# MLP down products of a two-layer decoder: pairs of output tiles by Strassen's seven block products over eight of eleven k tiles

## The chip, the cores and the metric

One core of one Trainium2 chip runs one program. The metric is the device time of one execution in microseconds (us), from the first to the last instruction of the program as the device counts it. All times of the kernel before are of this one core.

## The reference, cut to what matters

The reference is a decoder trunk of two layers over 512 tokens of width 1024, in float32: an RWKV-7 layer and a layer of dilated attention, each with a cross-attention to 256 memory tokens, and after each a gated MLP. The change touches only the MLP, and of it mainly the last line:

```python
u = rmsnorm(x, g) @ w_up                     # 1024 -> 2 x 2816
c = conv_b + sum(conv_w[j] * shift(u, j) for j in range(3))   # causal, width 3
gate, val = split(c, 2)
z = silu(gate) * val                          # 512 x 2816
x = x + z @ w_down                            # 2816 -> 1024
```

## The kernel before, in words

**Layout.** Activations lie with features on the 128 partitions and the 512 tokens along the free dimension. x is 8 tiles of 128x512. A weight tile of 128x128 is TensorE's stationary operand, a tile of activations the moving one.

**Precision.** TensorE's fast fp32r form rounds its operands. So every operand is split into a high part (rounded, written as fp32r) and a low part (what is left), and a product is three matmuls: high by high, high by low, low by high. ScalarE writes the high part (`copy`, L1332), VectorE the low part (`lower`, L1912: source minus high). For weights this is done tile by tile in two buffers, w_hi and w_lo.

**Stages.** The MLP of a layer (`mlp`) runs in two halves of 11 of the 22 feature tiles. Each half has an up stage and a down stage, so there are four of each in the program. In an **up stage** 11 pairs of tiles (gate and value) are made, each tile from 8 k tiles, 24 matmuls of 512 columns. `mlp_pairs` (L109) writes out pair 0 and the last two pairs (9 and 10) and runs the eight between them in a loop of four turns, two pairs a turn. For each tile VectorE multiplies the product by rstd into up_raw (L2239), ScalarE makes the conv's own tap (L1693), VectorE adds the two lagged taps (L2247); ScalarE takes SiLU of the gate; GpSimd multiplies (L2628, z_raw), or VectorE for pair 10 (L2254); ScalarE and VectorE split z into z_hi and z_lo. GpSimd does no more than that in these stages.

**Down stage.** 8 output tiles, one after the other, each the sum over 11 k tiles of 3 matmuls of 512 columns: 33 matmuls into one bank of PSUM. The banks 4 and 5 alternate. VectorE adds the bank into x (`residual`, L2204, signal x_up). A tile's weights are 128x1408; they are split by ScalarE and VectorE while TensorE works on the tile before. On TensorE this is a hardware loop of two turns over four tiles:

```python
for k in range(HALF):
    mm(o, w_hi[:, w, ks], z_hi[:, k, :], k == 0, False)
    mm(o, w_hi[:, w, ks], z_lo[:, k, :], False, False)
    q = mm(o, w_lo[:, w, ks], z_hi[:, k, :], False, k == HALF - 1)
```

**What sets the order.** Every engine has its own instruction queue, in the order written out by hand, and waits on semaphores (used: a ring tile has been multiplied; w_hi, w_lo; z_raw, z_hi, z; up_read; x_up). Raw weights come through a ring of four slots. SyncE (`one`, called by `stream`) issues the load of tile n when the low part of tile n-4 has been written. After the second half of layer 0 (stage 1 when counting from 0) the next layer's projection needs x scaled and split, so in that stage ScalarE (L1650, L1660) and VectorE (`gained_low`, L1937) have three more instructions for each tile of x, while GpSimd sums the squares (L2614).

Names used later: a *pair* of the down stage is two output tiles; a *stage* is a layer's half; `split(n)` is the splitting of ring tile n.

## Time and profile before

| | us |
|---|---|
| median of 3 runs | 1321.33 (1321.14 to 1321.41) |
| span of the profiled execution | 1319.1 |
| PE busy | 1288.5 (98%) |
| VectorE (DVE) busy | 806.7 (61%) |
| ScalarE (ACT) busy | 590.7 (45%) |
| GpSimd (POOL) busy | 375.0 (28%) |

The profiled execution's own time is not listed apart from its span; the median of the runs lies 2.2 us above that span. The views list instructions by engine: PE is the matmul, PEld the weight load. A row has the source line, the engine, the operation, out<-in by the program's names, partitions x elements, a count, and durations. A matmul's recorded duration holds its latency; matmuls overlap, so their spacing says more than their length. All matmuls of the helper `mm` have one line, L577.

### The profile page before, as it was taken

Reading aid. Unit: us, or ns where it says so; the run is one execution under the profiler, and the core shown is the slowest. Engines: PE = TensorE matmul, PEld = TensorE weight load, DVE = VectorE, ACT = ScalarE, POOL = GpSimd, SP = SyncE. Lnnn points to the kernel's source line nnn. Section 1 sums busy time; section 2 is a strip of 40 time slices with the busy share of each in tenths; the row PEclk is TensorE's granted clock in tenths of the full one; section 3 lists DMA queues with packets and bytes.
Section 4 is the critical chain, followed back from the end, with each engine's and each line's share of the span. In section 5 each row is a group of like instructions: output and inputs, shape, how many; then the busy total and the mean of one; then the engine's idle time right before and its main releaser. Section 6 shows DMA issues by size and latency. Waiting matters only on the chain.

```text
span 1319.1 us, 25215 instructions
## 1 busy us (share of the span) xinstructions
PE 1288.5 (98%) x10112; PEld 1023.9 (78%) x10112; DVE 806.7 (61%) x1142; ACT 590.7 (45%) x940; POOL 375.0 (28%) x342
## 2 busy tenths in 40 slices
PE   7999999999999999999999999998999999999999
PEld 5876777776478888888888887776778888888887
DVE  4777777786457665356674458538576662466642
ACT  6575645653244443124444455547554441244421
POOL 4469777774421110001101155330211100011100
PEclk9999999999999999999999999999999999999999
DMA  8100111114122333233332233120123332233331
GB/s 323 49 30 23 54 55 39 54 53 147 32 96 81 95 109 123 72 95 97 95 129 78 91 128 95 50 63 19 48 83 106 101 115 90 80 96 95 120 112 40
DMA packets 30042, 114.17 MB, mean 87 GB/s; under 512 B 3456, under 2 KB 5248, under 8 KB 29184
## 3 DMA queue, kind: packets, MB, share of 16 engines
q1 hardware_dynamic: 29952, 112.89, 26.1%
q8 instruction: 67, 1.10, 0.4%
q14 instruction: 23, 0.19, 0.1%
HBM read 110.78 MB, written 2.10 MB: 86 GB/s over the span
## 4 chain that ended last, share of the span: by engine, by line
PE 86%; DVE 5%; ACT 2%; issue 1%; POOL 0%; DVEq 0%; POOLq 0%; ACTq 0%
PE bank L577 84%; PE bank L1252 1%; DVE arena L1926 1%; ACT arena L1449 0%; PE bank L883 0%; DVE sin_part L2296 0%; DVE cos_part L2323 0%; DVE in_lo L1937 0%; PE bank L1136 0%; DVE head_stat L2306 0%; ACT w_hi L1332 0%; PE bank L1159 0%; DVE x L2204 0%; DVE stat L2004 0%; DVE cos_part L2292 0%
## 5 line engine op out<-in xcount | busy, mean ns | idle before, releaser
L1332 ACT ACTIVATE w_hi<-ring 128x1024 fp32r<-128x1024 f32 (+1 forms) x144 | 162.3, 1127 | 261.6 <-PE bank L577 261.6
L577 PE MATMUL bank<-in_hi,w_hi 128*128 128x512 f32 x704 | 274.9, 390 | 0.9 <-DVE in_lo L1937 0.9
L577 PE MATMUL bank<-in_hi,w_lo 128*128 128x512 f32 x704 | 273.9, 389 | 0.0
L577 PE MATMUL bank<-in_lo,w_hi 128*128 128x512 f32 x704 | 273.9, 389 | 0.0
L1912 DVE TENSOR_TENSOR w_lo<-ring,w_hi 128x1024 fp32r<-128x1024 f32 (+1 forms) x124 | 165.2, 1332 | 65.2 <-ACT w_hi L1332 64.8
L2628 POOL TENSOR_TENSOR z_raw<-silu,conv 128x512 f32<-128x512 f32 x40 | 51.5, 1289 | 537.8 <-DVE conv L2247 503.3
L577 PEld LDWEIGHTS bank<-in_hi,w_hi 128*128 128x128 f32 x704 | 132.1, 188 | 29.7 <-DVE in_lo L1937 1.3
L577 PEld LDWEIGHTS bank<-in_lo,w_hi 128*128 128x128 f32 x704 | 132.1, 188 | 27.7 <-issue 0.5
L577 PEld LDWEIGHTS bank<-in_hi,w_lo 128*128 128x128 f32 x704 | 132.1, 188 | 27.4
L577 PEld LDWEIGHTS bank<-arena 64*64 64x64 f32 (+2 forms) x4064 | 109.2, 136 | 49.7 <-issue 37.0
L2247 DVE SCALAR_TENSOR_TENSOR conv<-up_raw,par,conv 128x511 f32<-128x511 f32 (+1 forms) x176 | 131.8, 749 | 17.4 <-DVE conv L2247 9.8
L577 PE MATMUL bank<-arena 64*64 64x64 f32 (+4 forms) x4064 | 132.3, 239 | 6.9 <-DVE arena L1979 1.7
L577 PE MATMUL bank<-z_hi,w_hi 128*128 128x512 f32 x352 | 137.4, 390 | 0.1
L577 PE MATMUL bank<-z_lo,w_hi 128*128 128x512 f32 x352 | 137.0, 389 | 0.0
L577 PE MATMUL bank<-z_hi,w_lo 128*128 128x512 f32 x352 | 137.0, 389 | 0.0
L2204 DVE TENSOR_TENSOR x<-bank,x 128x512 f32<-128x512 f32 x48 | 33.1, 690 | 112.3 <-PE bank L577 112.3
L1912 DVE TENSOR_TENSOR z_lo<-z_raw,z_hi 128x512 f32 (+1 forms) x44 | 30.5, 692 | 97.8 <-ACT z_hi L1332 97.8
L1693 ACT ACTIVATE conv<-up_raw,par 128x512 f32<-128x512 f32 x88 | 71.2, 809 | 40.2 <-DVE up_raw L2239 39.8
L1332 ACT ACTIVATE z_hi<-z_raw 128x512 f32 (+1 forms) x44 | 27.8, 632 | 134.1 <-POOL z_raw L2628 123.2
L577 PEld LDWEIGHTS bank<-z_hi,w_hi 128*128 128x128 f32 x352 | 66.1, 188 | 15.4 <-DVE z_lo L1912 1.8
L577 PEld LDWEIGHTS bank<-z_hi,w_lo 128*128 128x128 f32 x352 | 66.1, 188 | 13.8
L577 PEld LDWEIGHTS bank<-z_lo,w_hi 128*128 128x128 f32 x352 | 66.1, 188 | 13.6
(280 smaller groups left out, 2150.5 us busy)
## 6 DMA issues: line engine op xcount, KB each, us to landing
ring<-w_ring SPq DMA_DIRECT2D x119, 512.0 KB, 3.5
ring<-w_ring SPq DMA_DIRECT2D x32, 704.0 KB, 4.1
ring<-w_pairs SPq DMA_DIRECT2D x18, 512.0 KB, 4.1
arena<-w_mem SPq DMA_DIRECT2D x2, 2048.0 KB, 19.1
arena<-w_ring SPq DMA_DIRECT2D x4, 512.0 KB, 4.4
x<-xT SPq DMA_DIRECT2D x1, 2048.0 KB, 7.8
outT<-x SPq DMA_DIRECT2D x8, 256.0 KB, 2.0
mask<-masks SPq DMA_DIRECT2D x1, 1536.0 KB, 7.2
```

Source lines behind the costliest of these rows:

```text
L577: return nc.tensor.matmul(out, lhsT, rhs, start=first, stop=last, skip_group_check=True)
L1252: m = nc.tensor.transpose(psum[:, 4:7, :].rearrange("p b t -> p (b t)")[:, at:at + P], sm[n % 3][:, b, q * P:(q + 1) * P], ident)
L1332: return nc.scalar.activation(out, in_, ACT.Copy)
L1693: nc.scalar.activation(conv[:, 2 * b + s, :], up_raw[:, 2 * b + s, :], ACT.Identity, scale=tap(l, tile, 2), bias=tap(l, tile, 3)).then_inc ...
L1912: V.tensor_tensor(dst, src, high.bitcast(F32), ALU.subtract).then_inc(sem(sig), 1)
L1926: V.reciprocal(rs, rs).then_inc(sem("hn_rc"), 1)
L2204: V.tensor_tensor(x[:, m, :], bank[out_bank(e, m)][:, :], x[:, m, :], ALU.add).then_inc(sem("x_up"), 1)
L2247: V.scalar_tensor_tensor(out=c[:, lag:T], in0=u[:, 0:T - lag], scalar=tap(l, 2 * p + (2 * HALF * half + s), 2 - lag), in1=c[:, lag:T], op0 ...
L2628: G.tensor_tensor(z_raw[:, b, :], silu[:, b, :], conv[:, 2 * b + 1, :], ALU.mult).then_inc(sem("z_raw"), 1)
```

## The change

The down stage handles its 8 output tiles in 4 pairs (o = 0..3). Of the 11 k tiles, pairs 1 to 8 of z form four groups of two; the plain ones (0, 9, 10) stay as they were. With two output tiles, two k tiles of a group and two halves of 256 tokens, the product is a 2x2 by 2x2 block product, made with seven block products (Strassen's scheme in Winograd's form) in place of eight:

- **Weights.** A11, A12, A21, A22 are blocks of 128x512 in the raw ring tiles (the host sorts each tile's k blocks as odd, even, plain). GpSimd forms S1 = A21+A22, S2 = S1-A11, S4 = A12-S2 and S3 = A11-A21 (`block_sum`), four 128x512 instructions a pair, after its z products of the up stage. Into `t_raw` go S1 and S2, into the idle half of `up_raw` S4 and S3.
- **Splitting.** Each of the seven weight blocks is copied by ScalarE and lowered by VectorE (512 columns) into one of four slots of w_hi and w_lo, plus once per pair the plain weights of both tiles (2x384 columns). Before it was 1408 columns per tile.
- **z.** In the up stage's loop VectorE forms the differences T1 to T4 per turn (three instructions), and ScalarE and VectorE split B11, B21, B22 and T1 to T4, each of 256 columns, in place of two tiles of 512.
- **TensorE.** Per pair: seven products of 4 x 3 matmuls of 256 columns, and two plain products of 3 x 3 of 512. All are written out, without a loop.
- **Adding up.** Products that go to several quarters of x pass through one half bank c, and VectorE adds it into 1, 3, 2 and 2 quarters (`stream_part`); the banks a and b are added whole (`stream_rest`). PE waits for the addition before it uses c again.
- **Buffers and signals.** conv, silu and z_raw move to other places in SBUF; some semaphores share a name now; the next stage's first two ring tiles are split at the end of the down stage. The squares of x for the projection are issued by `stream_high` and `stream_low`.

The diff, cut to its core:

```diff
+                    for o in range(4):
+                        a, b, c = (bank[i] for i in down_banks(g0, o))
+                        low, high = slice(0, TH), slice(TH, T)
+                        pe.wait_ge(sem("x_up"), KD * e + 2 * (o - 1) if o > 1 else KD * e)
+                        if o == 1:
+                            pe.wait_ge(sem("up_read"), 2 * (g0 + HALF))
+                        product(o, A11, c[:, low]).then_inc(sem("part_used"), 1)
+                        product(o, A12, a[:, low]).then_inc(sem("part_used"), 1)
+                        product(o, S4, a[:, high], True).then_inc(sem("part_used"), 1)
+                        pe.wait_ge(sem("accumulated"), added(stage, o, 1))
+                        product(o, S2, c[:, low], True).then_inc(sem("part_used"), 1)
+                        plain(o, 0).then_inc(used, 1)
+                        pe.wait_ge(sem("accumulated"), added(stage, o, 2))
+                        product(o, S1, c[:, low]).then_inc(sem("part_used"), 1)
+                        plain(o, 1)
+                        pe.wait_ge(sem("x_up"), KD * e + 2 * o + 1)
+                        product(o, S3, c[:, low]).then_inc(sem("part_used"), 1)
+                        product(o, A22, b[:, low], True).then_inc(used, 1)
```

with `product` waiting for the low part of its block and issuing, for each of the four groups,

```diff
+                            mm(out, hi[:, ks], z[:, 0, at], j == 0 and not adds, False)
+                            mm(out, hi[:, ks], z[:, 1, at], False, False)
+                            q = mm(out, lo[:, ks], z[:, 0, at], False, j == ZP - 1)
```

VectorE in the last pair of an up stage, and in the down stage:

```diff
+                        if last:
+                            read(0)
+                            plain_low(0)
+                            lagged(0, 1)
+                            lagged(0, 2)
+                            z_low(p - 1, q - 1)
+                            block_low(0, A11)
+                            block_low(0, A12)
+                            read(1)
+                            block_low(0, S4)
+                            lagged(1, 1)
+                            block_low(0, S2)
+                            stream_part(0, A11)
+                            lagged(1, 2)
+                            block_low(0, S1)
...
+                            z_low(p, q)
+                            return
...
+                    for o in range(4):
+                        if o:
+                            stream_part(o, A11)
+                            block_low(o, S1)
+                        block_low(o, S3)
+                        block_low(o, A22)
+                        if o:
+                            stream_low(2 * o - 1)
+                        stream_part(o, S2)
+                        if o < 3:
+                            block_low(o + 1, A11)
+                        stream_rest(o, 0)
+                        stream_part(o, S1)
+                        if o < 3:
+                            block_low(o + 1, A12)
+                            stream_low(2 * o)
+                            stream_part(o, S3)
+                            block_low(o + 1, S4)
+                            stream_rest(o, 1)
+                            block_low(o + 1, S2)
+                            plain_low(o + 1)
+                    stream_low(KD - 2)
+                    stream_part(3, S3)
+                    split(down + KD)
+                    stream_rest(3, 1)
+                    stream_low(KD - 1)
+                    split(down + KD + 1)
```

GpSimd, behind all its z products of the stage:

```diff
+                        if i == S1:
+                            if o:
+                                pool.wait_ge(sem("part_lo"), part_count(stage, o - 1, S1))
+                            else:
+                                pool.wait_ge(sem("z"), z_count(stage, 2, ZP - 1, 2))
+                            a, b, op = a21, a22, ALU.add
...
+                        G.tensor_tensor(sum_raw(g0, i), a, b, op).then_inc(sem("weights_formed"), 1)
+
+                    for o in range(4):
+                        for i in (S1, S2, S4, S3):
+                            block_sum(o, i)
```

VectorE at the end of each turn of the up loop (second pair of the turn):

```diff
+                        V.tensor_tensor(t_raw[:, 0:2, :], z_raw[:, :, TH:T], z_raw[:, 0, :].rearrange("p (a t) -> p a t", t=TH),
+                                        ALU.subtract).then_inc(sem("formed"), 1)
+                        dve.wait_ge(sem("formed"), t_count(stage, j, 1))
+                        V.tensor_tensor(t_raw[:, 2, :], b22, t_raw[:, 0, :], ALU.subtract).then_inc(sem("formed"), 1)
+                        dve.wait_ge(sem("formed"), t_count(stage, j, 2))
+                        V.tensor_tensor(t_raw[:, 3, :], b21, t_raw[:, 2, :], ALU.subtract).then_inc(sem("formed"), 1)
...
+                        if q == 2:
+                            z_sums(p, j)
+                            z_low(p, q, j)
+                            z_sums_low(j)
```

## Rows read from the trace of the kernel before

**Rows 1.** The page: head, busy times, the chain that ended last by line.

```profile
span 1319.1 us, 25215 instructions
...
PE 1288.5 (98%) x10112; PEld 1023.9 (78%) x10112; DVE 806.7 (61%) x1142; ACT 590.7 (45%) x940; POOL 375.0 (28%) x342
...
PE bank L577 84%; PE bank L1252 1%; DVE arena L1926 1%; ACT arena L1449 0%; PE bank L883 0%; DVE sin_part L2296 0%; DVE cos_part L2323 0%; DVE in_lo L1937 0%; PE bank L1136 0%; DVE head_stat L2306 0%; ACT w_hi L1332 0%; PE bank L1159 0%; DVE x L2204 0%; DVE stat L2004 0%; DVE cos_part L2292 0%
```

**Rows 2.** Busy times by window, two of the four down stages.

```profile
core 0: us, PE busy (x) PEld busy (x) DVE busy (x) ACT busy (x) POOL busy (x), PEclk, DMA share, GB/s
506.20:566.40 60.20, 60.17 (x265) 49.48 (x265) 20.94 (x20) 12.60 (x11) 0.00 (x0) 1.00 0.28 90
686.10:746.30 60.20, 60.17 (x266) 49.51 (x265) 28.45 (x27) 27.26 (x25) 7.78 (x6) 1.00 0.24 80
```

**Rows 3.** Timeline of PE: down stage 0, then narrow matmuls early in the program.

```profile
start us, us, engine line op out<-in xcount [idle before <-releaser]
506.24 0.39 PE L577 MATMUL bank<-z_hi,w_hi 128*128 128x512 f32 x1
...
513.23 0.50 PE L577 MATMUL bank<-z_hi,w_hi 128*128 128x512 f32 x1
...
559.15 0.39 PE L577 MATMUL bank<-z_lo,w_hi 128*128 128x512 f32 x1
...
566.18 0.39 PE L577 MATMUL bank<-z_hi,w_lo 128*128 128x512 f32 x1
...
39.75 1.84 PE L577 MATMUL bank<-cst,arena 128*128 128x2 f32 x16
41.46 6.72 PE L577 MATMUL bank<-arena 128*128 128x256 f32 x30
```

**Rows 4.** Groups of instructions over the whole span, shapes apart: VectorE, GpSimd, ScalarE.

```profile
line engine op names shapes xcount | busy us, mean ns | idle before us <-releasers
L2247 DVE SCALAR_TENSOR_TENSOR conv<-up_raw,par,conv 128x511 f32<-128x511 f32 x88 | 65.8, 747 | 6.8 <-ACT conv L1693 5.9
L1912 DVE TENSOR_TENSOR w_lo<-ring,w_hi 128x1408 fp32r<-128x1408 f32 x32 | 52.0, 1626 | 38.8 <-ACT w_hi L1332 38.8
L1912 DVE TENSOR_TENSOR z_lo<-z_raw,z_hi 128x512 f32 x32 | 22.2, 692 | 77.8 <-ACT z_hi L1332 77.8
...
L2628 POOL TENSOR_TENSOR z_raw<-silu,conv 128x512 f32<-128x512 f32 x40 | 51.5, 1289 | 537.8 <-DVE conv L2247 503.3 <-ACT silu L1696 34.5
...
L1332 ACT ACTIVATE z_hi<-z_raw 128x512 f32 x32 | 20.2, 632 | 102.8 <-POOL z_raw L2628 102.8
```

**Rows 5.** Timelines of VectorE and GpSimd: end of up stage 0, end of down stage 0.

```profile
490.99 0.69 DVE L1912 TENSOR_TENSOR z_lo<-z_raw,z_hi 128x512 f32 x1 [2.42 <-ACT z_hi L1332]
491.60 0.68 DVE L2239 TENSOR_TENSOR up_raw<-bank,rstd 128x512 f32<-128x512 f32 x1
492.20 1.22 DVE L1912 TENSOR_TENSOR w_lo<-ring,w_hi 128x1024 fp32r<-128x1024 f32 x1
...
506.44 0.69 DVE L2239 TENSOR_TENSOR up_raw<-bank,rstd 128x512 f32<-128x512 f32 x1 [0.59 <-PE bank L577]
...
560.56 1.23 DVE L1912 TENSOR_TENSOR w_lo<-ring,w_hi 128x1024 fp32r<-128x1024 f32 x1 [0.74 <-ACT w_hi L1332]
...
499.52 1.29 POOL L2628 TENSOR_TENSOR z_raw<-silu,conv 128x512 f32<-128x512 f32 x1 [9.45 <-DVE conv L2247]
```

**Rows 6.** Timelines of VectorE and GpSimd where both work at once.

```profile
366.44 0.68 DVE L2204 TENSOR_TENSOR x<-bank,x 128x512 f32<-128x512 f32 x1
...
370.84 1.78 DVE L1937 SCALAR_TENSOR_TENSOR in_lo<-x,par,in_hi 128x512 fp32r<-128x512 f32 x1
...
376.07 0.75 DVE L1937 SCALAR_TENSOR_TENSOR in_lo<-x,par,in_hi 128x512 fp32r<-128x512 f32 x1
...
798.61 4.88 DVE L2323 TENSOR_TENSOR cos_part<-cos_part,sin_part 128x512 f32<-128x512 f32 x3
...
366.33 1.34 POOL L2614 TENSOR_TENSOR y<-y 128x512 f32<-128x512 f32 x1 [0.80 <-ACT y L1666]
...
370.63 1.44 POOL L2614 TENSOR_TENSOR y<-y 128x512 f32<-128x512 f32 x1 [0.80 <-ACT y L1666]
376.10 1.86 POOL L2614 TENSOR_TENSOR y<-y 128x512 f32<-128x512 f32 x1 [4.03 <-ACT y L1666]
```

**Rows 7.** Groups in down stage 1 (690 to 747 us), then the page's ring loads.

```profile
L1937 DVE SCALAR_TENSOR_TENSOR b_lo<-x,par,b_hi 128x512 fp32r<-128x512 f32 x7 | 7.8, 1121 | 0.0
...
L1650 ACT ACTIVATE b_hi<-x,par 128x512 fp32r<-128x512 f32 x7 | 8.4, 1207 | 26.5 <-DVE x L2204 26.5
...
ring<-w_ring SPq DMA_DIRECT2D x32, 704.0 KB, 4.1
```

More of the change, by code:

```diff
@@ L74 @@
 UPS = 2 * HALF
+ZP = 4
+ZC = HALF - 2 * ZP
+TH = T // 2
+PARTW = 7 * TH
+ZW = ZP * PARTW + ZC * T
+BLOCKW = ZP * P
+CONVW = ZC * P
+B11, B21, B22, T1, T3, T2, T4 = range(7)
+A11, A12, S4, S2, S1, S3, A22 = range(7)
+MOVING = B11, B21, B22, T2, T1, T3, T4
+ZN = HALF + 2 * ZP
 U_QM0, U_MK0, U_MK1, U_END = 0, 2, 4, 6
@@ L149, in tensor @@
             return group.enter_context(nc.sbuf_tensor(name, shape, dt))
+        with ExitStack() as mlp_work:
+            conv = tensor(mlp_work, "conv", [P, 4, T])
+            silu = tensor(mlp_work, "silu", [P, 2, T])
+            z_raw = tensor(mlp_work, "z_raw", [P, 2, T])
         y = sb("y", [P, KD, T])
@@ new lines, in plain @@
+                    def plain(o, s):
+                        out = bank[down_banks(g0, o)[s]][:, :]
+                        pe.wait_ge(sem("part_lo"), part_count(stage, o, None))
+                        for k, p in enumerate((0, HALF - 2, HALF - 1)):
+                            if o == 0:
+                                pe.wait_ge(sem("z"), z_count(stage, p))
+                            ks = slice(k * P, (k + 1) * P)
+                            first = s == 1 and k == 0
+                            mm(out, plain_slot(w_hi_all)[:, s, ks], z_plain(0, p), first, False)
+                            mm(out, plain_slot(w_hi_all)[:, s, ks], z_plain(1, p), False, False)
+                            q = mm(out, plain_slot(w_lo_all)[:, s, ks], z_plain(0, p), False, k == ZC - 1)
+                        return q
@@ L1701, in mlp, with gate @@
-                    squares(down, 3 * l + 1 + half, 1)
+                        def gate():
+                            act.wait_ge(sem("conv_gate"), p + (g0 + 1))
+                            nc.scalar.activation(silu[:, b, :], conv[:, 2 * b, :], ACT.Silu).then_inc(sem("silu"), 1)
+                        if last:
+                            plain_high(0)
+                            own_tap(0)
+                            block_high(0, A11)
+                            block_high(0, A12)
+                            gate()
+                            block_high(0, S4)
+                            own_tap(1)
+                            block_high(0, S2)
+                            block_high(0, S1)
+                        else:
+                            for s in range(2):
+                                split_at(p, up + 2 + s, q)
+                                if half == 0 and q == 0 and s == 0:
+                                    stream_root(2 * l + 1)
+                                own_tap(s)
+                            gate()
@@ new lines, in stream_rest, with stream_low @@
+                    def stream_rest(o, s):
+                        dve.wait_ge(used, down + 2 * o + s + 1)
+                        dve.wait_ge(sem("accumulated"), added(stage, o, 4 if s else 2))
+                        m = 2 * o + s
+                        V.tensor_tensor(x[:, m, :], bank[down_banks(g0, o)[s]][:, :], x[:, m, :], ALU.add)                            .then_inc(sem("x_up" if s else "accumulated"), 1)
+                    def stream_low(m):
+                        if e == 2:
+                            gained_low(G_ATTN1, m, 2 * KD + 1)
@@ L2617, in mlp, with up_pair @@
                 for half in range(2):
+                    up, down = mlp_tiles(l, half)
                     g0 = FT * l + HALF * half
-                    def up_pair(p, q):
+                    stage = 2 * l + half
+                    def up_pair(p, q, j):
                         if q == HALF - 1:
```

344 lines of the change are left out of this document (254 added, 90 removed).

## The prediction

> **What bounds the kernel now.** I read the head of the page and its chain first: TensorE is busy for 98% of the span, and matmuls recorded at L577 alone hold 84% of the chain that ended last [rows 1]. The change touches the four down stages (layer by half). The windows over two of them last 60.20 us, PE busy throughout at granted clock 1.00 (the level of 2.4 GHz), while VectorE is busy for 21 to 28 us and GpSimd for 0 to 8 [rows 2]; the other two read like the first. So I ask what one matmul costs on PE, not how long it is recorded: 0.39 us is recorded, but 31 of them lie between 559.15 and 566.18, one every 0.2268 us [rows 3]. A stage is 8 tiles x 33 x 0.2268 = 59.9 us, and 0.3 us is lost once where its loop is entered (the row at 513.23 is late). Everything outside PE is hidden in these stages, with much slack. The change spends that slack.
>
> The profiled execution spans 1319.1 us; the runs' median is 1321.3, so 2.2 us lie around the span and I add them at the end.
>
> **1. Fewer columns on PE.** Removed: 4 x 8 x 33 = 1056 matmuls of 512 columns, 239.5 us. Added: 16 pairs x 7 products x 4 k x 3 = 1344 of 256 columns, and 16 x 2 x 3 x 3 = 288 of 512 for the three plain k tiles, 65.3 us. No row shows an fp32r matmul of 256 columns. At half of 0.2268 it would cost 0.113. Below, it can't pass the weights, since each matmul loads 128x128: sixteen matmuls of 2 columns take 1.84 us, which is (1.84-0.25)/15 = 0.106 each [rows 3]. At 2.4 GHz 512 columns are 0.2133 us of streaming, so 0.0135 are something else; if that something is fixed, 256 columns cost 0.107+0.0135 = 0.120. The 29 steps of the plain f32 form at 256 columns are (6.72-0.38)/29 = 0.219 each [rows 3], the upper bound if the fp32r form loses its speed at this width. I take **0.118**, nearer to the fixed case: 158.6+65.3-239.5 = -15.6 us, and -1.2 us for the four loop entries that are unrolled: **-16.8**. The equal point is (239.5-65.3)/1344 = 0.1296. So 9% fewer columns (960 against 1056 times 512) give 7% of the stages' time, as the fixed part of each matmul is kept and there are more of them.
>
> The Trainium skill (TensorE: Matmul & The Clock Gate, Back-to-back issue gap) gives N/2.4 + 2.5 ns, so an estimate of 109 ns for 256 columns and -28 us for this part. By that formula 512 columns take 216 ns, where the trace shows 227, so I don't use it for this data type.
>
> **2. The start of a stage.** Take the stage's first possible matmul as zero (506.24 in the trace). VectorE reads a tile's product 0.2 us after its last matmul (506.44), so the last but one (24 x 0.2268 = 5.44 us earlier) is read at -5.2. GpSimd ends the z product of pair 9 at 500.81, that is -5.4 [rows 5]. Only behind that instruction stand GpSimd's four weight sums for the first output pair, 128x512 each, by the row of z_raw 1.29 us [rows 4]: 5.2 us. At the same time VectorE has to do, in this order, the low part of the plain weights (768 columns, by the 1408-column row some 0.90), two conv taps (0.67 each), z's low part and the first block's low part (0.61 each; back to back an instruction costs 0.08 less than its length, 490.99 to 491.60): 3.5 us. All have two operands in SBUF.
> That matters because of the clash of the two engines [rows 6]. VectorE's conversion issued at 370.84 while GpSimd was working to 372.07 took 1.78 us and not 0.75: it ran after GpSimd had ended. The other way round GpSimd's sum issued at 376.10, with VectorE working to 376.82, took 1.86 and not 1.29. Three VectorE products at 798.61 take 4.88 us beside a GpSimd instruction each. An addition whose one operand is in PSUM runs at 0.68 beside GpSimd (366.44). So the two queues of SBUF work add up: 5.2+3.5-5.4 = 3.2 us after zero, less some 0.15 at each of five hand-overs, plus a signal: the first product starts **2.3 us late**. Below: 0, if they don't add up. Above: 3.2. The Trainium skill (SBUF — State Buffer, Who interferes with whom) says this of two SBUF inputs against a reading GpSimd, and that the loser blocks for the whole instruction. Strictly applied, without my 0.15, its estimate is 5 us more over the kernel; the trace shows GpSimd waiting 0.57 where 0.72 were left.
>
> **3. The middle of the first pair.** The sixth step on PE (S1's product) reuses the half bank that VectorE must first add into x (the addition of S2's product, three quarter tiles, about 0.85 us). On VectorE's queue stand ahead of it: the last conv tap, S1's low part, the last z product, z's low part (behind ScalarE's 0.63), the low parts of S3 and A22. Without GpSimd the addition ends some 1.1 us after PE wants it. But S1's low part also frees the buffer for GpSimd's sums of the second pair, which start right then, and z's low part, S3's and A22's are each put behind one: 3 x 1.29 + 3 x 0.61 from about 7.2 is 12.9, less the hand-overs 12.5, the addition to 13.4, a signal 13.6. PE stands there from 2.3 + 48 x 0.118 + 9 x 0.2268, with 0.3 for z, 10.3. **3.3 us late**; bounds 1.1 and 3.8. PE never regains this, as it has no slack: 4 x (2.3+3.3) = **+22.4**.
>
> **4. Later pairs.** A pair is 84 x 0.118 + 18 x 0.2268 = 14.0 us of PE. VectorE's list is 7 low parts (4.3), the plain one (0.9), four additions (2.4) and two full ones (1.2): 8.8, and GpSimd's 5.2 fall on at most four of these. The S2 addition is due 2.0 us after S2's product ends. In three stages it about meets that (0.3 late in two pairs: **+1.5** with both). In stage 1 (layer 0, second half) VectorE has b_lo (1.12) and ScalarE b_hi and another instruction (1.21 for b_hi) per tile besides [rows 7]; b_lo also waits behind a sum, and pairs 1 and 2 are 2.3 late, pair 3 (no sums left) 0.4: **+5.0**. Bounds 1.2 and 6.
>
> **5. The end of a stage.** Before, the next tile's low weights were ready at 561.8 for a start at 566.4 [rows 5]. Now the conversion stands behind the addition of S3's product, which ends 1.4 us before the pair does: +0.2 signal, 0.61 addition, 1.13+ conversion, signal: 0.6 late, in three stages (the last has no successor): **+1.9**. x's last tile is final 0.7 us after PE, as before, so the output is unchanged.
>
> **6. The up stages.** Per two pairs of 21.8 us VectorE gets three differences and two more low parts, some 2.4 us. They lie ahead of reading the next product: it was read at 491.60 and the weights for 495.36 were ready at 493.4 [rows 5]; 1.9 us later that is 495.3. It just fits: **+0.5** over 16 turns, bounds 0 and 4. The split of ring tiles, the DMA queue (same bytes, two tiles of a pair freed together early in the pair, 4.1 us to land [rows 7]) and PE's waits on semaphores already met cost nothing: tile boundaries in the trace show none, and there are at least 9 us between freeing and use. If that cover went, GpSimd's sums would be late by what is missing.
>
> Sum: -16.8+22.4+1.5+5.0+1.9+0.5 = **+14.5**, so a span of 1333.6 and a time of **1335.8 us**. Where ends lie far apart (0 or 3.2, 1.1 or 3.8) I stand near the clash's full price, since three rows at different places show it.
>
> **The rivals.**
> *Little clash* (faster). If GpSimd's sums are short holds, or fall beside PSUM-sided work, parts 2 and 3 are 1.1 us a stage and part 4 is 1.2: -16.8+4.4+1.2+1.9 = -9.3, **1312 us**. For it: the order on VectorE has PSUM additions between the low parts. Against: the clash as measured [rows 6].
> *Cheap narrow matmul, clash as above.* At 0.109 part 1 is 12 us better: **1324 us**. For it: the floor of 0.106. With little clash too it is 1300.
> *Strict blocking*, at 0.120: 14.5+2.7+4.7, **1343 us**.
> *The narrow form loses its speed*: 1344 x 0.219 for 158.6, +136, **1472 us**. Only the plain f32 row speaks for it.
> That the change doesn't do what it says (seven products of half width) would show in the count of matmuls; I see no way to it, as each product is written out.
>
> **Chances.** Forecast 0.45, little clash 0.20, both cheap 0.05, cheap matmul with clash 0.12, strict 0.15, lost speed 0.03. The measurement tells 0.2% (2.6 us) from no change. Faster: 0.20+0.05 and a little of the third, 0.27. Within: half of the third, 0.06. Slower: 0.67. The range leaves out both ends, some 0.2, mostly 1300 and 1472: 1309 to 1348. Likeliest case alone: 1329 to 1342.
>
> **What would show it.** In the changed profile: matmuls of 128x256 spaced 0.118 (0.113 to 0.120); the down windows 62 to 64 us and 66 to 69 in stage 1; waits of PE on the additions into x, 3 us each, four times, and on the first low block at each stage's start; GpSimd's sums and VectorE's low parts well above 1.29 and 0.69. Wrong it is if windows are under 59 us, if the low parts keep 0.69 beside the sums, or if the spacing is over 0.13.

## The result and the profile after

The changed kernel takes 1352.2 us (median of 4 runs, 1351.2 to 1353.0) beside 1321.2 us (1321.0 to 1321.4): a ratio of 1.0234, 95% interval 1.0219 to 1.0248. It is 31 us slower. The forecast was 1335.8 us with a range to 1348: the sign was right, the size half of what came. Its profiled execution spans 1350.1 us (1319.1 before), so everything below is read against +31.0 us.

Head and chain of the page of the changed kernel, to be read against [rows 1]:

```profile
span 1350.1 us, 27158 instructions
...
PE 1288.6 (95%) x10688; PEld 1046.5 (78%) x10688; DVE 962.9 (71%) x1382; ACT 644.8 (48%) x1068; POOL 475.3 (35%) x406
...
PE 49%; DVE 26%; issue 8%; ACT 6%; POOL 4%; DVEq 1%; ACTq 1%; POOLq 0%
```

The same last line, the chain by engine, of the kernel before:

```profile
PE 86%; DVE 5%; ACT 2%; issue 1%; POOL 0%; DVEq 0%; POOLq 0%; ACTq 0%
```

TensorE has 576 matmuls more, yet is busy for the same time and a smaller share of the span. VectorE, which held 5% of the chain, now holds 26% of it.

The four down stages by window in the changed kernel (the start of each one's first product to the next up stage's); two of them stood at 60.20 us with clock 1.00 in [rows 2]:

```profile
core 0: us, PE busy (x) PEld busy (x) DVE busy (x) ACT busy (x) POOL busy (x), PEclk, DMA share, GB/s
509.81:572.03 62.22, 59.19 (x408) 54.99 (x409) 47.23 (x60) 20.69 (x32) 18.44 (x12) 0.97 0.25 81
695.05:765.57 70.52, 61.23 (x408) 56.04 (x408) 56.91 (x67) 34.40 (x45) 28.25 (x18) 0.95 0.21 71
1098.50:1162.26 63.76, 59.51 (x409) 54.92 (x409) 47.20 (x60) 20.46 (x32) 18.41 (x12) 0.97 0.25 79
1285.32:1346.70 61.38, 60.12 (x407) 56.09 (x408) 45.95 (x58) 19.27 (x30) 18.45 (x12) 0.95 0.23 78
```

They are 17.2 us longer together (257.9 us for 4 x 60.17); the wait of 3.15 us ahead of each is not even in them (12.6 us), and 1.2 us are spread over the rest. VectorE went from 21 to 47 us in stage 0, and the granted clock is under 1.00 in all four: that had not been forecast.

What VectorE and GpSimd did around the start of down stage 0 in the changed kernel (timeline), TensorE's first product behind them:

```profile
498.61 1.53 DVE L2516 SCALAR_TENSOR_TENSOR conv<-up_raw,par,conv 128x511 f32<-128x511 f32 x2
...
502.99 2.10 DVE L2111 TENSOR_TENSOR w_lo<-ring,w_hi 128x768 fp32r<-128x768 f32 x1 [0.89 <-ACT w_hi L1456]
505.01 3.45 DVE L2516 SCALAR_TENSOR_TENSOR conv<-up_raw,par,conv 128x511 f32<-128x511 f32 x2
...
516.93 1.78 DVE L2111 TENSOR_TENSOR w_lo<-up_raw,w_hi 128x512 fp32r<-128x512 f32 x1
518.63 1.76 DVE L2111 TENSOR_TENSOR w_lo<-ring,w_hi 128x512 fp32r<-128x512 f32 x1
520.32 0.94 DVE L2459 TENSOR_TENSOR x<-bank,x 128x768 f32<-128x768 f32 x1
...
501.51 1.30 POOL L2990 TENSOR_TENSOR t_raw<-ring 128x512 f32<-128x512 f32 x1
502.98 1.30 POOL L2990 TENSOR_TENSOR t_raw<-t_raw,ring 128x512 f32<-128x512 f32 x1 [0.17 <-POOL t_raw L2990]
504.75 1.50 POOL L2990 TENSOR_TENSOR up_raw<-ring,t_raw 128x512 f32<-128x512 f32 x1 [0.46 <-POOL t_raw L2990]
506.21 1.71 POOL L2990 TENSOR_TENSOR up_raw<-ring 128x512 f32<-128x512 f32 x1
...
509.81 0.77 PE L661 MATMUL bank<-z,w_hi 128*128 128x256 f32 x2 [3.00 <-DVE w_lo L2111]
510.38 0.42 PE L661 MATMUL bank<-z,w_lo 128*128 128x256 f32 x1
...
521.32 0.50 PE L661 MATMUL bank<-z,w_hi 128*128 128x256 f32 x2 [2.06 <-DVE x L2459]
```

Two conv taps that take 1.53 us back to back one up tile earlier take 3.45 beside GpSimd's sums; the low parts at 516.93 and 518.63 take 1.78 and 1.76 instead of 0.69. TensorE stands for the first low part (509.81) and for the addition of S2's product (521.32), the two places that the prediction named.

A third thing was new: the clock. Windows of the changed kernel before, in and behind two drops of it:

```profile
506.80:509.60 2.80, 0.02 (x1) 0.00 (x0) 2.77 (x4) 1.10 (x2) 1.12 (x1) 1.00 0.00 0
509.80:512.90 3.10, 3.09 (x14) 3.10 (x15) 2.81 (x5) 1.42 (x3) 0.00 (x0) 0.50 0.00 0
513.20:516.20 3.00, 3.00 (x28) 3.00 (x27) 2.30 (x5) 1.11 (x3) 1.33 (x1) 1.00 0.01 3
703.90:707.10 3.20, 0.57 (x4) 0.57 (x5) 3.20 (x4) 0.00 (x0) 2.84 (x2) 1.00 0.66 236
707.60:710.90 3.30, 3.30 (x12) 2.82 (x11) 1.88 (x4) 2.11 (x3) 0.00 (x0) 0.50 0.51 184
711.10:714.00 2.90, 2.90 (x24) 2.78 (x23) 1.43 (x2) 1.20 (x2) 0.00 (x0) 1.00 0.00 0
```

TensorE stood still for some 3 us, then worked at 0.50 of its clock, the level of 1.2 GHz (at once in the first case, after 1.0 us at full clock in the second), and later at 1.00 again: 14 matmuls in 3.1 us, where 28 fit into 3.0 at full clock. There are five such stretches (from 509.6, 707.5, 724.6, 1110.3 and 1284.4). Their matmuls come every 0.213 us (256 columns) and 0.427 us (512), and the excess over 0.120 and 0.227 sums to 8.8 us over the five (I first took it for 10, and the expectations below say so). Whether these 9 us were in the time remained to be tested.

### The profile page after: what moved, and what is told of

The parts are those of the page before. It is cut to its first block, busy times and chain, and to the rows that moved or that the text cites. A ratio compares the mean times of both kernels' runs of the same rounds, so it can differ in the third digit from the quotient of the medians.

```text
span 1350.1 us, 27158 instructions
## 1 busy us (share of the span) xinstructions
PE 1288.6 (95%) x10688; PEld 1046.5 (78%) x10688; DVE 962.9 (71%) x1382; ACT 644.8 (48%) x1068; POOL 475.3 (35%) x406
## 4 chain that ended last, share of the span: by engine, by line
PE 49%; DVE 26%; issue 8%; ACT 6%; POOL 4%; DVEq 1%; ACTq 1%; POOLq 0%
PE bank L661 47%; DVE conv L2516 7%; DVE w_lo L2111 7%; POOL z_raw L2961 3%; ACT conv L1845 3%; DVE up_raw L2508 3%; DVE z L2111 2%; ACT w_hi L1456 1%; DVE x L2459 1%; DVE t_raw L2488 1%; PE bank L1376 1%; DVEq L2516 1%; DVE t_raw L2491 1%; DVE arena L2125 1%; ACT arena L1573 0%
## 5 line engine op out<-in xcount | busy, mean ns | idle before, releaser
L661 PE MATMUL bank<-z,w_hi 128*128 128x256 f32 (+1 forms) x1088 | 230.7, 311 | 28.1 <-DVE x L2459 16.1
L1456 ACT ACTIVATE w_hi<-ring 128x1024 fp32r<-128x1024 f32 (+2 forms) x176 | 161.0, 918 | 193.0 <-PE bank L661 193.0
L661 PEld LDWEIGHTS bank<-z,w_hi 128*128 128x128 f32 x1088 | 180.9, 198 | 42.9 <-DVE x L2459 21.6
L2111 DVE TENSOR_TENSOR w_lo<-ring,w_hi 128x1024 fp32r<-128x1024 f32 (+2 forms) x156 | 179.2, 1151 | 46.6 <-ACT w_hi L1456 45.4
L661 PE MATMUL bank<-z,w_lo 128*128 128x256 f32 (+1 forms) x544 | 167.7, 308 | 0.0
L661 PEld LDWEIGHTS bank<-z,w_lo 128*128 128x128 f32 x544 | 107.5, 198 | 4.2
L2508 DVE TENSOR_TENSOR up_raw<-bank,rstd 128x512 f32<-128x512 f32 x88 | 60.4, 686 | 31.4 <-PE bank L661 31.4
L3017 POOL TENSOR_TENSOR w_lo<-ring,w_hi 128x1024 fp32r<-128x1024 f32 x20 | 48.5, 2426 | 84.1 <-ACT w_hi L1456 84.1
L2459 DVE TENSOR_TENSOR x<-bank,x 128x256 f32<-128x256 f32 (+1 forms) x64 | 43.9, 687 | 40.6 <-PE bank L661 40.5
L1456 ACT ACTIVATE arena<-bank 128x512 f32<-128x512 f32 (+1 forms) x72 | 40.9, 585 | 64.9 <-PE bank L661 52.5
```

The costliest lines, as they stand in the source:

```text
L661: return nc.tensor.matmul(out, lhsT, rhs, start=first, stop=last, skip_group_check=True)
L1456: return nc.scalar.activation(out, in_, ACT.Copy)
L2111: V.tensor_tensor(dst, src, high.bitcast(F32), ALU.subtract).then_inc(sem(sig), 1)
L2459: V.tensor_tensor(to, c.to_broadcast([P, {A11: 1, S2: 3, S1: 2, S3: 2}[i], TH]), to, ALU.add) .then_inc(sem("x_up" if i == S1 else "accumu ...
L2508: V.tensor_tensor(up_raw[:, 2 * b + s, :], bank[2 * b + s][:, :], rstd[:, :], ALU.mult).then_inc(sem("up_read"), 1)
L3017: G.tensor_tensor(w_lo[:, n % 2, 0:w], ring[:, n % SLOTS, 0:w], w_hi[:, n % 2, 0:w].bitcast(F32), ALU.subtract).then_inc(sem("w_lo"), 1)
```

## The experiments

The theory that I began with: VectorE and GpSimd exclude each other on SBUF, that makes VectorE late for TensorE, and the waits bring the clock down. The rivals: VectorE's queue is too long or badly ordered whatever GpSimd does; the narrow products by themselves cost clock.

### The sums cut to one column

```diff
-G.tensor_tensor(sum_raw(g0, i), a, b, op)
+G.tensor_tensor(sum_raw(g0, i)[:, 0:1], a[:, 0:1], b[:, 0:1], op)
```

> This kernel leaves out the weight sums: each of GpSimd's 16 sums a stage is cut to one column, with its waits and signals kept. Theory (GpSimd's sums and VectorE's two-operand work on SBUF exclude each other, and that makes VectorE late for TensorE): VectorE's pair of conv taps at the start of a down stage goes back from 3.45 to about 1.53 us and the rest's low part from 2.10 to about 0.94, so the first product's low part is ready 3.1 us earlier and the 3.15 us gap of TensorE at each start is nearly gone (four times, -12.6); the two low parts ahead of S2's addition go back from 1.78 and 1.76 to 0.69 each, so the gap before product S1 of the first pair falls by 2.2 us to 0, 1.2, 1.2 and 0 (-7.7), those of stage 1's pairs 1 and 2 by as much (-4.4). No gap of 3 us is left, so the granted clock is 1.00 throughout (-10). Sum about 1318 us, 1313 to 1322. Rival (VectorE's own order and length of queue, whatever GpSimd does): the gaps fall by less than a third, the clock still drops, about 1342 us. Rival (the clock goes down because of the 256-column products, not because of gaps): gaps gone but clock still at 0.95 to 0.97 in the down stages, about 1328 us.

1318.3 us, 0.9978 of before (0.9968 to 0.9988), clock 1.00. VectorE's operations in down stage 0 (groups with shapes apart, 498 to 565 us), the changed kernel first, this one second:

```profile
L2111 DVE TENSOR_TENSOR w_lo<-ring,w_hi 128x512 fp32r<-128x512 f32 x12 | 12.1, 1013 | 0.8 <-ACT w_hi L1456 0.7
L2459 DVE TENSOR_TENSOR x<-bank,x 128x512 f32<-128x512 f32 x6 | 4.2, 692 | 7.3 <-PE bank L661 7.3
```

```profile
L2111 DVE TENSOR_TENSOR w_lo<-ring,w_hi 128x512 fp32r<-128x512 f32 x12 | 8.2, 687 | 2.4 <-ACT w_hi L1456 2.2
L2459 DVE TENSOR_TENSOR x<-bank,x 128x512 f32<-128x512 f32 x8 | 5.5, 691 | 11.9 <-PE bank L661 11.9
```

With two operands in SBUF a low part falls from 1013 to 687 ns; the addition with one operand in PSUM is 692 and 691 with or without the sums. The start gap is gone in all four stages. In each first pair 1.11 us is left, where the prediction said "Without GpSimd the addition ends some 1.1 us after PE wants it". The sums cost 34 us, through other engines' waits. The length of the queue alone is refuted as the cause, and so is a price of narrow products in clock. That the number was met within 1 us is in part luck: the expectation had 10 us for the clock, which is worth 3.3 (next experiment), and against that the waits in the middle of the first pairs fell by 9.4 us and not 7.7, and those of 0.36 us in later pairs (2.2 us in all) and 1.6 us of gaps under 0.25, which it didn't count, went too. The Trainium skill (SBUF — State Buffer, Who interferes with whom) holds this exclusion for VectorE work with two SBUF inputs against a GpSimd operation that reads SBUF; the rows agree.

### TensorE kept at work in the waits

hold(out, n) issues n products of 128x512 into a bank that the next product starts anew.

```diff
+if o == 0:
+    hold(c, 12)
 product(o, A11, c[:, low])
...
+if o == 0 or (stage == 1 and o < 3):
+    hold(b, 4 if stage == 3 else 8)
 pe.wait_ge(sem("accumulated"), added(stage, o, 2))
```

> The changed kernel with TensorE kept at work in the gaps: 12 products of 128x512 into a bank that the next product starts anew ahead of each down stage's first product (12 x 0.227 = 2.7 of the 3.15 us gap), and 8 (4 in stage 3) ahead of S1 of the first pair, and of pairs 1 and 2 in stage 1 (1.8 us of gaps of 1.0 to 3.4). Nothing else changes, and the waits still end when they did. Theory (the clock falls after a stretch in which TensorE stood still): granted clock 1.00 in all four down stages and about 10 us less, 1342 us (1340 to 1345), with the same moments at which the waits end. Rival (the clock falls because of the stretches of 256-column products themselves, or because of the total load): clock as before at 0.95 to 0.97, time 1352 or more. Rival (half clock is only how the trace shows late weight parts): the spacing of 0.21 us stays, 1352.

1348.9 us, 1.021 of before (1.0193 to 1.0227); clock 1.00 throughout. So the drop follows standing still, not narrow products. But it saved 3.3 us, not 10, and not the 8.8 of the spacing. Its down stages by window:

```profile
510.10:572.47 62.37, 59.90 (x417) 55.08 (x417) 47.33 (x60) 20.46 (x32) 18.44 (x12) 1.00 0.25 81
695.52:763.25 67.73, 63.79 (x433) 57.96 (x433) 57.14 (x67) 34.42 (x45) 28.35 (x18) 1.00 0.23 75
1096.16:1158.51 62.35, 59.90 (x416) 55.07 (x417) 47.32 (x60) 20.46 (x32) 18.43 (x12) 1.00 0.25 81
1281.61:1343.07 61.46, 58.69 (x411) 54.20 (x412) 46.02 (x58) 18.93 (x30) 18.41 (x12) 1.00 0.24 78
```

Stages 0 and 3 are as long as with half clock, stage 1 is 2.8 and stage 2 1.4 us shorter. In stages 0 and 3 the clock fell at the stage's start, ahead of the wait for S2's addition: that wait was 2.2 and 1.0 us there, and is 3.5 and 3.4 here. VectorE ends the addition when it ends it, and a slow TensorE merely arrived later. In stages 1 and 2 the clock fell behind that wait, and there it was paid.

### The narrow form alone

The kernel before, with each product of a down stage as two of 256 columns. It starts the second half of a bank between two products of the first, and what it adds up is not the reference's sum: only its time is used here.

```diff
+for h in range(2):
+    t = slice(h * T // 2, (h + 1) * T // 2)
+    mm(o[:, t], w_hi[:, w, ks], z_hi[:, k, t], k == 0, False)
...
```

> The kernel before, with each 512-column product of the down stages issued as two of 256 columns; same work for all other engines. Measures the price of the narrow form by itself: 4 stages x 264 = 1056 products that become 2112, each pair 2 x 0.120 instead of 0.2267, so +14.0 us: 1335.3 us (1334 to 1337) at a granted clock of 1.00. By the prediction's price of 0.118 it would be +9.8 us, 1331. Rival (narrow products by themselves cost clock): clock under 1.00 in the down stages and 1340 or more.

1333.8 us, +12.4; clock 1.00. A stage is 63.35 us for 528 products: 0.1200 each, and with twice the matmuls no loss of 0.3 us at the loop's entry any more. So 512 columns are 0.2133 + 0.0135 and 256 are 0.1067 + 0.0133: the fixed part is fixed. The prediction had named 0.120 for that case and took 0.118. By the formula that the Trainium skill gives for the gap of a single matmul (TensorE: Matmul & The Clock Gate, Back-to-back issue gap) an estimate would be 0.109; the measured 0.120 decides for fp32r here.

### S2's addition ahead of two low parts

```diff
+stream_part(o, S2)
 block_low(o, S3)
 block_low(o, A22)
 ...
-stream_part(o, S2)
```

> The changed kernel with one step of VectorE moved: the addition of S2's product comes ahead of the low parts of S3 and A22 instead of behind them. Theory (TensorE's wait in mid pair is for this addition, held up by two low parts that clash with GpSimd): the gaps before S1 of the first pairs (2.2, 3.4, 3.4, 1.0 us) and of stage 1's pairs 1 and 2 (2.4 each) go to about 0, those of later pairs (0.36) too, -16 us at most; the three drops of the clock that followed them go as well (-6). S3's and A22's low parts come 0.9 us later, while S3 is due 3.5 us after S1's start, so up to 1 us a pair of that comes back in the first pairs. 1332 us (1328 to 1338). The start gaps of 3.15 us stay. Rival (the low parts themselves are what is late, in whatever order): the gap moves to the wait before S3, about 1348 to 1352.

1350.5 us, a miss by 18, and what the rival had said. The wait ahead of S1 went to nothing, and one ahead of S3's product came: 1.0 us in the first pairs of stages 0 to 2 and 2.0 in stage 3's, 0.9 in later pairs (0.36 before), 3.0 and 4.0 in stage 1. S3's product reuses the same half bank, and S1's addition that frees it now stood behind the same two stretched low parts. The wait had moved and not shrunk: 2.9 us in stage 0 before (2.22 and twice 0.36) and after (1.04 and twice 0.92).

### The rest of the first pair earlier

In the last up pair on VectorE, and the high part on ScalarE alike:

```diff
+plain_low(0)
 read(0)
-plain_low(0)
```

> The changed kernel with one piece moved: the high and low part of the first pair's rest weights (128x768) are formed one pair of up tiles earlier, ahead of ScalarE's z copy and ahead of VectorE's read of the last pair's first up tile, where VectorE stood idle for 1.28 us. Theory (VectorE is short of time between the last two up tiles, by what GpSimd's sums add to it): the 2.10 us operation and the 0.89 us wait ahead of it leave the chain to the first product, which also has to take in that ScalarE's own tap comes 0.3 us later; the start gap falls from 3.15 to 1.0 us (0.5 to 1.5) in each stage, -8.6 us. The gap in the middle of the first pair stays within 1 us of 2.2 to 3.4, as VectorE's chain behind it moves by as much as TensorE does. 1343 us (1340 to 1347). Rival (the start waits for the landing of the weights or for ScalarE): the start gap stays over 2.5 us, 1350.

1349.7 us; the start gap fell from 3.15 to 2.9 us, not to 1.0. VectorE and GpSimd in this kernel (timelines):

```profile
500.41 0.95 DVE L2112 TENSOR_TENSOR w_lo<-ring,w_hi 128x768 fp32r<-128x768 f32 x1
...
503.92 3.62 DVE L2517 SCALAR_TENSOR_TENSOR conv<-up_raw,par,conv 128x511 f32<-128x511 f32 x2 [1.48 <-ACT conv L1845]
507.46 1.75 DVE L2112 TENSOR_TENSOR z<-z_raw,z 128x512 fp32r<-128x512 f32 x1
...
500.63 1.89 POOL L2962 TENSOR_TENSOR z_raw<-silu,conv 128x512 f32<-128x512 f32 x1 [9.95 <-DVE conv L2517]
```

The moved low part met GpSimd's z product instead (1.89 us, not 1.29), the sums came 0.4 to 0.6 later against TensorE, and the stretch went to z's low part (1.75, not 0.69). VectorE also stood idle for 1.48 us ahead of the taps, for ScalarE's own tap, which came behind a copy of the late z. My expectation had taken the stretched length off; only the unstretched 0.95 was VectorE's own. The rival had the time, 1350, and part of the reason: ScalarE is in this chain.

### All sums on VectorE

> The changed kernel with all 64 weight sums done by VectorE, in its queue at the nearest place: two ahead of the first read of the last up pair, two behind A12's low part, and the four of each later pair behind S2's addition. VectorE gets 64 x 0.69 = 44 us more to do; GpSimd has nothing left in the down stages, so no operation of VectorE is stretched. Theory (it is the exclusion, not the amount of work): start gap from 3.15 to under 0.5 us (the pair of taps 3.45 to 1.53, the rest's low part 2.10 to 0.94, the two sums ahead partly in idle time), mid gap of the first pair no larger than 2, clock 1.00; 1325 us (1316 to 1334). Rival (VectorE's queue is simply too long, so that 2.76 us more of it in each pair must make it worse): over 1352 us, with start gaps of 3 us and over and gaps of over 2 us in every pair. The count without the exclusion is close in the pairs: about 7 low parts x 0.69 + 0.98 + 4.1 for the additions + 2.76 = 12.7 of 14.16 us.

1338.5 us, clock 1.00, a miss by 13; VectorE gets 44 us more to do and the kernel is 14 us faster. VectorE's busy time hardly moved (962.9 us in the changed kernel, 964.7 here, 921.3 with sums of one column): the time that it stands blocked by GpSimd is recorded as busy, and these 42 us were of the size of the work that came in. The start gap is 0.43 us. Three stages hold 4.3 to 5.0 us of waits over 0.25 and stage 1 10.5: the order was naive. The exclusion is shown, and so is that a second limit stands close behind it.

### New orders

Sums on GpSimd, two of the first pair's ahead of the z product of the last but one pair, the rest of the first pair early, and in the pairs and at the end:

```diff
+stream_part(o, S2)
 block_low(o, S3)
+stream_rest(o, 0)
+stream_part(o, S1)
 block_low(o, A22)
...
-stream_part(o, S2)
...
-stream_rest(o, 0)
-stream_part(o, S1)
...
+split(down + KD)
 stream_part(3, S3)
-split(down + KD)
```

> The changed kernel with its orders changed and nothing else: the rest of the first pair one up pair earlier; GpSimd's first two sums ahead of the z product of the last but one pair (it stood idle for 9.9 us there); in the pairs VectorE adds S2's product first, then does S3's low part, the addition of the first output tile, S1's addition, and only then A22's low part; at the end the next up tile's low part comes ahead of S3's addition. Sums stay on GpSimd. Theory: start gap under 1 us (-9 or more), gap ahead of S1 gone, that ahead of S3 (1.0 in the first pairs when only S2's addition was moved) gone too; but each pair has about 13.4 us of VectorE work with the stretching against 14.16 us of TensorE, and stage 1 has 1.4 us more of it, so stage 1 stays short by 0.5 to 1 us a pair. 1323 us (1318 to 1332). Rival (the stretched low parts are late in any order, as when S2's addition alone was moved): 1340 or more.

1325.8 us, 1.0033 of before (1.002 to 1.0046). Three down stages are 57.2 us with no wait over 0.25; stage 1 is 63.2. The start gap, expected under 1, is 1.75 us, and another of 0.8 came in the up stage. So most of what the sums cost in the pairs had been order after all: additions that free a bank stood behind low parts that nobody yet needed.

> Both together: the orders of the kernel with changed orders, and all 64 sums on VectorE, spread over the pair where nothing is due (S1's behind the addition of the first output tile, S2's and S4's behind A22's low part, S3's behind the addition of the second; for the first pair two in the idle time ahead of the last up pair). Theory (exclusion and order are all that stood between the change and its gain): start, middle and end gaps under 0.5 us each, clock 1.00, down stages of 57.3 to 58 us against 60.2: 4 x -2.5 = -10 us against the kernel before, 1312 us (1309 to 1319). Rival (VectorE with 13 of 14.2 us of work a pair is late in one place or another, and every wait for it costs): 1322 or more.

1322.2 us, 1.0007 (0.9998 to 1.0016), a miss by 10, and the rival's time: no gap at the start, but 1.0 ahead of S4 in each stage, three stages of 58.7, and stage 1 at 64.7.

### A11 and A12 ahead of the taps

> The changed kernel with one step of the last up pair moved, on ScalarE and VectorE: the parts of A11 and A12 are formed ahead of the taps of the last pair's first up tile instead of behind them; the rest of VectorE's queue, and its sum of work, stay. Theory (VectorE's chain through the last up pair and the first down pair is one chain, and the waits at the start and in mid pair are two places at which TensorE meets it): the start gap of 3.15 us falls to under 0.5, but the later steps of the chain come no sooner, so that TensorE waits ahead of S4, S2, the last z or S1 for what it saved; per stage the first pair ends at the same moment within 0.7 us. 1350 us (1347 to 1353). Rival (the gaps add up, and each can be taken away by itself): 4 x 3.1 = 12 us less, 1340 us.

1357.2 us: the theory's places held, its time did not. The start gap went from 3.15 to 0.3, and the addition of S2's product in stage 0 is at 520.23, where it was at 520.32: VectorE's chain through the last up pair and the first down pair is one, and moving TensorE's meeting points along it gains nothing. TensorE now waits ahead of S4 (1.8), S2 and the last z (1.0) and S1 (3.4). That it became 5 us slower is again the clock: in stage 0 the drop now lies behind the last of these waits (520.6 to 527.4). S1's product starts 0.1 us sooner than in the changed kernel, and the stage ends 2.8 us later.

### The best of both, and stage 1

The first pair's sums on VectorE, the others on GpSimd, A11's and A12's parts ahead of the taps.

> The two rearranged kernels joined, each where it had the shorter gaps: the first pair's four sums on VectorE (the kernel with all sums there had no gap at the start of a stage, the one with GpSimd's had 1.7 and 0.8), those of pairs 1 to 3 on GpSimd (down stages of 57.2 us there, against 58.7). In the last up pair A11's and A12's parts now come ahead of the taps, S4's low part right behind the read of the last up tile, since the kernel with all sums on VectorE waited 1.0 us there. Theory (what is left is VectorE's exclusion by GpSimd and its order): three down stages of 57.3 us, stage 1 with 1.4 us more of VectorE work in a pair 62 to 63 us, up stages as before + 0.2: 3 x 57.3 + 62.5 - 4 x 60.17 + 0.8 = -5.5 us, 1316 us (1313 to 1320), clock 1.00 save after a gap in stage 1. That would be faster than the kernel before. Rival (the part that VectorE has to do in the last up pair is too much in any order, and the wait goes to S4, S2 or the last z): 1 us or more in the first pair of each stage, 1321 or more.

1320.5 us, 0.9997 (0.9988 to 1.0006), no difference from the kernel before and a miss by 4.5, of which stage 1 has 2.2 (64.7 us for 62.5) and the three others 1.7. Stages 0 and 1 by window:

```profile
506.50:564.37 57.87, 57.45 (x409) 53.59 (x408) 45.16 (x61) 21.17 (x33) 16.62 (x12) 1.00 0.29 89
684.25:748.97 64.72, 59.05 (x409) 53.87 (x407) 57.41 (x68) 35.57 (x47) 27.66 (x18) 1.00 0.24 78
```

Three stages win 2.3 us each; stage 1, with b_lo on VectorE and b_hi and squares on ScalarE, gives 4.6 back.

The same kernel with b_lo moved, in stage 1:

```diff
 block_low(o, S1)
+if o == 3:
+    stream_low(1)
+    stream_low(2)
...
 block_low(o, A22)
-if o:
-    stream_low(2 * o - 1)
+if o == 3:
+    stream_low(4)
+    stream_low(5)
```

> The joined kernel (first pair's sums on VectorE, the others on GpSimd, new orders) with one thing moved in stage 1 alone: the low parts of the next layer's input (b_lo, 1.16 us each on VectorE, only in that stage) that stood in pairs 1 and 2 come in pair 3, where VectorE has no low parts of a next pair to form. Nothing is left out. Theory (stage 1 took 64.7 us against 57.9 of the others because 2.3 us more of VectorE's work in a pair is more than the pair holds): stage 1 falls to 58.5 us (58 to 60), 6 us less: 1314.5 us (1312 to 1317), which is faster than the kernel before by 0.5%. Rival (the loss in stage 1 is of the whole stage's work, or of ScalarE's b_hi and squares, which stay): stage 1 stays over 62 us, 1318 or more.

1319.8 us, 0.9987 (0.9978 to 0.9996): faster than before by 0.13%, less than the 0.2% that I had called measurable at the start, though the interval of 11 runs excludes 1. Stage 1 fell from 64.7 to 63.7 only: the rival held in its time. Its last wait, 2.2 us, ends with the next tile's low part, which stood behind b_lo instructions that ran for 4.17 us. VectorE and ScalarE at this place (timelines):

```profile
742.13 4.17 DVE L2137 SCALAR_TENSOR_TENSOR b_lo<-x,par,b_hi 128x512 fp32r<-128x512 f32 x3
746.23 1.21 DVE L2112 TENSOR_TENSOR w_lo<-ring,w_hi 128x1024 fp32r<-128x1024 f32 x1
...
741.64 1.22 ACT L1774 ACTIVATE b_hi<-x,par 128x512 fp32r<-128x512 f32 x1 [6.18 <-DVE x L2487]
```

VectorE works without a break here, and the last of the three b_lo takes 2.04 us and not 1.15, issued while GpSimd summed squares. ScalarE had stood idle for 6.18 us, waiting for VectorE's addition.

The kernel with the new orders and its sums cut to one column:

> This kernel leaves out the weight sums (one column each, waits and signals kept) and has the new orders of the last up pair, the pairs and the end: what the 256-column form could give at most, if the sums cost nothing. Theory (narrow products at 0.120 us, 1632 in place of 1056 of 0.2267, and nothing else in TensorE's way): down stages of 57.2 us, stage 1 of 58 to 60; 3 x 57.2 + 59 - 240.7 = -10.1, + 0.8 in the up stages: 1312 us (1310 to 1315), clock 1.00. Rival (ScalarE's or the ring's timing sets a wait of its own that the sums had covered): over 0.5 us of gaps in each stage's first pair, 1316 or more.

1311.2 us, 0.9922 (0.9906 to 0.9937), as expected. Windows of stages 0 and 1:

```profile
506.11:562.91 56.80, 56.80 (x410) 53.80 (x409) 39.21 (x59) 20.61 (x32) 2.59 (x12) 1.00 0.28 91
682.79:742.22 59.43, 57.44 (x410) 53.87 (x408) 48.77 (x66) 35.28 (x46) 11.18 (x18) 1.00 0.26 85
```

This is the most that the form could give here: 3.4 us in each of three stages and 0.7 in stage 1, and it takes sums that cost nothing.

## Why the forecast had the sign and not the size

By the prediction's own steps; the waits are read from the kernel with TensorE kept at work, where the clock doesn't blur them.

| step | forecast | measured |
|---|---|---|
| 1 fewer columns | -16.8 | -13.5 |
| 2 start, four times | 2.3 each, +9.2 | 3.15 each, +12.6 |
| 3 middle of the first pair | 3.3 each, +13.2 | 3.46 each, +13.8 |
| 4 later pairs | +1.5 and +5.0 | +2.2 and +6.0 |
| 5 end | +1.9 | +2.2 |
| 6 up stages | +0.5 | +0.8 |
| clock | none | +3.6 |

The measured column sums to +27.7 of 31.0. Another 2.6 lie in gaps under 0.25 us between products, 0.5 to 0.7 a stage (stage 0 kept at work is 62.37, of which 56.80 are step 1's, 3.46 the wait for S1, 0.72 two later ones and 0.73 the end); the last 0.7 are outside the MLP's stages. Against the forecast's +14.5 the miss is 16.5 us, and no single step carries it: the clock 3.6, step 2 3.4, step 1 3.3, the small gaps 2.6, steps 3 to 6 together 2.9, the rest 0.7.

- **Step 1** took 0.118 for a product that costs 0.120 (1344 x 0.002 = 2.7 us), though its own argument gave 0.120: "if that something is fixed". The other 0.6 are 0.15 us a stage beside the products. Measured where nothing is in the way, a stage is 56.80 for 60.17, four times -3.4.
- **Step 2** is, of the terms in the sum, the one that was short by most: "the first product starts **2.3 us late**". It was 3.15, the 3.2 that the same step had as its strict bound. Part of this is the step's own arithmetic: 3.2 less five times 0.15 is 2.45, and with a signal (0.2 in step 5) 2.65. For the other 0.5 the overlap of "some 0.15 at each of five hand-overs" is what failed: in its place the chain has losses. GpSimd's four sums took 6.4 us and not 5.2 (501.51 to 507.92), since dependent ones start 0.17 to 0.46 us after one another and two were stretched, and its z product came 0.3 us later against TensorE's end than before.
- **Step 3** holds as a wait, with and without GpSimd (3.46 for 3.3, 1.11 for 1.1), but not as a moment. It has S1's product start 13.6 us after the stage's first possible matmul; it starts at 14.7 (521.32 less 506.66). TensorE's arrival (at 11.3 for 10.3, with matmuls in the waits) and VectorE's addition were both about 1 us later than forecast, and the difference stayed. The run with A11 and A12 ahead of the taps shows why steps 2 and 3 are one term: without the start gap the addition ends where it did. What was short is that chain, by 1.1 us in each stage.
- **Steps 4 to 6** hold in place and are each a little short, all in one direction. Every one assumed that VectorE arrives just in time; that this is the reason was not tested. (0.3 us in two pairs of three stages is 1.8, too, and not 1.5.)
- **The clock was missing** from the sum, the largest single part of the miss, and no reason was given for leaving it out. The steps had TensorE standing for 2 to 3 us eight times and priced its work behind that at full speed. Its price is not the 8.8 us that spacing gives but 3.3 of time (3.6 of span), since a drop ahead of a wait is absorbed by it.

The rival *strict blocking* (1343) came nearest; with the clock's 3.3 it gives 1346, within 6 us. The cases that the prediction put outside its range (1300 and 1472) had 0.08 of the chance, not the 0.2 that it speaks of. *Little clash* (1312) is refuted by the kernel without sums: 1318.3 even then. What fell among my later reasons: that the exclusion alone stood between the change and its gain. Order alone brought 26 of the 31 us back with the sums still on GpSimd (with the clock, as the long waits went), and taking the sums out alone brought 34: the two are not to be added, as a stretched low part costs nothing where nobody waits behind it. And the gain itself is small: 13.5 us at most, of which stage 1's own load on VectorE and ScalarE takes 2.6 even with free sums.

Open: what stage 1 could still give. At its end the rows of the last version point at VectorE's queue, a b_lo stretched by GpSimd's squares included, and not at ScalarE's b_hi and squares (1.2 and 1.1 us per tile), which waited for VectorE; but no run changed either alone. A version that leaves stage 1 in the old form wasn't tried.

## What to carry to other kernels

A product form that saves TensorE columns is paid in VectorE and GpSimd work and in waits on bank reuse: count a pair's full list on the helper engine against TensorE's shorter pair, with every overlap of two-SBUF-operand work added in series, before counting columns. Order that list by who waits: additions that free a bank first, operands of the next pair last. And find the chain: a step moved within it only moves the wait; work has to leave it.

## What the runs showed of the hardware

- The fp32r product has a fixed 13.3 to 13.5 ns beside its streaming: 0.1200 us at 256 columns (528 of them in 63.35 us), 0.2268 at 512.
- Waits of TensorE of 2.2 to 3.4 us inside otherwise full stages were followed by the 1.2 GHz level in five of nine cases of the changed kernel's execution (two of four at the starts, three of five in the stages), and which starts it was varied between kernels that shared them. In later kernels a wait of 2.1 us (new orders, stage 1) and one of 2.2 (last version, end of stage 1) were followed by it, and one of 2.1 (joined kernel) was not. With matmuls in the waits it didn't happen; after the waits of 1.1 us and less in the kernel without sums neither.
- A drop of the clock can cost nothing: stages 0 and 3 were as long with one as without (62.2 and 62.4 us, 61.4 and 61.5).
- GpSimd loses too: its difference of two ring slices took 1.73 us on average beside VectorE, where sums that met nothing or had started first took 1.29 to 1.30.
- Time that VectorE stands blocked by GpSimd counts as busy in the profile: 962.9 us with GpSimd's sums, 921.3 with sums of one column.
